# The place of projected tiles reused for residual rows, FFN weights and normed rows, and the second norm's tiles transposed by DMA instead of TensorE

## What is computed

```python
h_stream = h_stream + rms_norm(merged @ w_o[l], g_mix_post[l])
# ---- channel-mixing sub-layer: SwiGLU (sandwich norm) ----
h = rms_norm(h_stream, g_ffn_pre[l])
gate, up = jnp.split(h @ w_ffn_in[l], 2, axis=-1)
f = (jax.nn.silu(gate) * up) @ w_ffn_out[l]
h_stream = h_stream + rms_norm(f, g_ffn_post[l])
```

## Time and profile before

| | us |
|---|---|
| median of 3 runs (lowest, highest) | 1818.75 (1818.65, 1823.68) |
| the profiled execution's own time | 1814.77 |
| its span on the slowest core, core 2 | 1813.7 |
| PE busy in the span | 1747.8 (96%) |
| DVE, ACT, POOL busy | 692.9, 520.6, 122.1 |
| span of the fastest core, core 4 | 1797.7 |

### The profile page before, as it was taken

The page is one execution under the profiler, slowest core; times in us unless marked ns, Lnnn a source line. Parts: engine busy times, 40 slices in busy tenths (PEclk is TensorE's granted clock), DMA queues, the critical chain, the costliest instruction groups (busy, mean ns, idle before and its releaser), DMA issues.

```text
span 1813.7 us, 25284 instructions; the slowest of 8 cores (1797.7 to 1813.7 us)
## 1 busy us (share of the span) xinstructions
PE 1747.8 (96%) x9598; PEld 847.2 (47%) x9760; DVE 692.9 (38%) x825; ACT 520.6 (29%) x970; POOL 122.1 (7%) x262
## 2 busy tenths in 40 slices
PE   5999999999999989999899999999999999999998
PEld 3755555544444434444444444444444444444443
DVE  4666878967885634526610110101010110101023
ACT  5755566376547530024410000000000000101010
POOL 2000000000000011100000000000000000000000
PEclk9999999999999999999999999999999999999999
DMA  9753444466667889946954446455554431434456
GB/s 236 218 133 81 83 77 90 70 124 134 122 124 154 177 158 224 239 93 177 231 110 81 70 75 115 75 103 98 96 102 76 80 66 33 96 64 76 84 145 229
DMA packets 89239, 218.55 MB, mean 120 GB/s; under 512 B 34400, under 2 KB 35040, under 8 KB 83840
## 3 DMA queue, kind: packets, MB, share of 16 engines
q0 software_dynamic: 31744, 121.71, 39.5%
q1 hardware_dynamic: 54208, 90.06, 16.8%
q10 hardware_dynamic: 3168, 5.15, 0.8%
HBM read 302.28 MB, written 36.24 MB: 187 GB/s over the span
## 4 chain that ended last, share of the span: by engine, by line
PE 81%; DMA 10%; DVE 3%; issue 3%; SPq 2%; ACT 1%; ACTq 0%; DVEq 0%; POOLq 0%
PE ps L224 80%; DMA xin<-xseq 3%; DMA yr<-yc_d 3%; SPq L218 2%; DMA wr<-w_in 2%; DMA xr<-xseq 1%; DVE xs L251 1%; PE ps L232 1%; DVE ptmp L248 1%; DMA gT<-g_d 0%; ACT xs L242 0%; DVE os L251 0%; DMA g_d<-go 0%; DVE xg L251 0%; ACT xg L242 0%
## 5 line engine op out<-in xcount | busy, mean ns | idle before, releaser
L224 PE MATMUL ps<-hN,wf 128*128 128x512 bf16 x2759 | 606.8, 380 | 4.6 <-DVE hN L266 0.9
L224 PEld LDWEIGHTS ps<-hN,wf 128*128 128x128 bf16 x2816 | 275.8, 98 | 334.8 <-issue 4.3
L224 PE MATMUL ps<-hT,wr 128*128 128x512 bf16 (+1 forms) x1884 | 371.0, 350 | 8.6 <-DMA wr<-w_in 5.5
L224 PE MATMUL ps<-wfo,agr 128*128 128x512 bf16 x1379 | 302.5, 379 | 1.5
L248 DVE TENSOR_TENSOR agr<-ps,sgt 128x512 bf16<-128x512 f32 x88 | 60.8, 691 | 534.3 <-PE ps L224 530.9
L224 PEld LDWEIGHTS ps<-hT,wr 128*128 128x128 bf16 x1920 | 179.9, 97 | 176.0 <-issue 11.1
L224 PEld LDWEIGHTS ps<-wfo,agr 128*128 128x128 bf16 x1408 | 137.8, 98 | 166.1
L242 ACT ACTIVATE sgt<-ps 128x512 f32<-128x512 f32 x88 | 52.4, 597 | 537.9 <-PE ps L224 537.9
L224 PE MATMUL ps<-wo,mgd 128*128 128x512 bf16 x500 | 111.0, 379 | 2.0 <-ACT sg L244 0.9
L248 DVE TENSOR_TENSOR facc<-ps,gp2a 128x512 f32<-128x512 f32 x24 | 16.6, 692 | 212.2 <-ACT sqj L242 212.2
L242 ACT ACTIVATE sqj<-ps 128x512 bf16<-128x512 f32 x32 | 19.1, 597 | 271.5 <-PE ps L224 271.5
(11 more groups left out here) (152 smaller groups left out, 1367.9 us busy)
## 6 DMA issues: line engine op xcount, KB each, us to landing
wf<-w_ffn_in POOLq DMA_DIRECT2D x88, 512.0 KB, 5.8
wr<-w_in POOLq DMA_DIRECT2D x52, 512.0 KB, 6.0
wfo<-w_ffn_out POOLq DMA_DIRECT2D x16, 1408.0 KB, 9.6
xin<-xseq SPq DMA_DIRECT2D x15, 1024.0 KB, 8.4
wo<-w_o POOLq DMA_DIRECT2D x16, 512.0 KB, 14.2
yr<-yc_d SPq DMA_DIRECT2D x32, 256.0 KB, 11.1
xr<-xseq SPq DMA_DIRECT2D x16, 512.0 KB, 7.7
hs_d<-os SPq DMA_DIRECT2D x8, 1024.0 KB, 8.7
```

The costliest lines, as they stand in the source:

```text
L224: return lambda e: e.matmul(o, lhsT=l, rhs=r, start=st, stop=sp)
```

## The change

`mgd` is laid out by token tile, [128, 8, 16, 128], and known to the scheduler as eight regions `mg0` to `mg7`, so that the place of one token tile comes free when that tile is projected. A second residual buffer `xr1` takes the place of `mg0` and `mg1`, a third buffer of normed rows `xg2` that of `mg4`, two FFN weight buffers that of `mg2` and `mg3`, two more that of `gpost`. Of the nine `wf` buffers the first six loads take `wf5, wf6, wf3, wf4, wf7, wf8`, and the later ones `wf0` to `wf4` in turn. Token tile 7 uses `os3` instead of `os2`. The 16 TensorE transposes, the ACT copy and the DVE copy of each token tile are replaced by one DMA on SP's queue with `transpose=True`, for all eight tiles.

```diff
+FLIPPED = 8
...
+    def flip(self, out, in_, nbytes, slot, reads, writes):
+
+        self.add("sp", [lambda e: e.dma_start(out=out, in_=in_, transpose=True)], 0.4, reads, writes, dma=1.5 * nbytes, slot=slot)
...
-    mgd = S.tile("mgd", [128, 16, NTOK], BF16, 82112)
+    mgd = S.tile("mgd", [128, 8, 16, 128], BF16, 82112, parts=("mg", 8))
...
-            S.stt(mgd[:, m, cs], t[:], 0.5, YR[yi][:], ALU.mult, ALU.add, 512, [tk, "yr%d" % yi], [("mgd", m, blk)])
+            four = lambda v: v.rearrange("p (a n) -> p a n", a=4)
+            S.stt(mgd[:, 4 * blk:4 * blk + 4, m, :], four(t[:]), 0.5, four(YR[yi][:]), ALU.mult, ALU.add, 512, [tk, "yr%d" % yi],
+                  [("mg%d" % (4 * blk + i), m) for i in range(4)])
...
-    xr = S.tile("xr", [128, D], F32, 196800)
-    XG = [S.tile("xg%d" % i, [128, D], BF16, a) for i, a in enumerate((204992, 52288))]
+    XR = [S.tile("xr%d" % i, [128, D], F32, a) for i, a in enumerate((196800, 82112))]
+    XG = [S.tile("xg%d" % i, [128, D], BF16, a) for i, a in enumerate((204992, 52288, 98496))]
...
-        xg, xk = XG[(t + 1) % 2], "xg%d" % ((t + 1) % 2)
+        oi = 3 if t == 7 else t % 5
+        os_, ok = OS[oi], "os%d" % oi
+        xi = (1, 0, 1, 0, 2, 1, 0, 2)[t]
+        xg, xk = XG[xi], "xg%d" % xi
...
-        if t + 1 < 8:
-            load_r(t + 1)
+        if t + 2 < 8:
+            load_r(t + 2)
...
+        if t < FLIPPED:
+            S.flip(hN[:, :, 128 * t:128 * t + 128], xg[:], 524288, xk, [xk], [("hN", t, 0), ("hN", t, 1)])
+            return
         for h in range(2):
...
+    load_r(1)
     for t in range(8):
         if t >= 3 and t + 2 < 8:
...
-    WF = [S.tile("wf%d" % i, [128, 16, 128], BF16, 35904 + 4096 * i) for i in range(5)]
+    WF = [S.tile("wf%d" % i, [128, 16, 128], BF16, a) for i, a in enumerate((52288, 35904, 40000, 44096, 48192, 90304, 94400, 164032, 168128))]
...
-        i = fr[0] % 5
+        n = fr[0]
+        i = (5, 6, 3, 4, 7, 8)[n] if n < 6 else (n - 6) % 5
         fr[0] += 1
-        S.dma("pool", flat(WF[i][:]), src, 1048576, "wf%d" % i, writes=[("wf%d" % i,)])
+        S.dma("pool", flat(WF[i][:]), src, 1048576, "wf%d" % i, reads=[("hN", 2, 0)] if n < 6 else [], writes=[("wf%d" % i,)])
```

More of the change, by code:

```diff
@@ L66, in __init__, with region, tile @@
         self.sub = None
-    def tile(self, name, shape, dtype, addr):
+    def region(self, name, lo, hi):
+        self.inherit[name] = [n for (n, a, b) in self.tiles if a < hi and lo < b]
+        self.touch[name] = set()
+        self.tiles.append((name, lo, hi))
+    def tile(self, name, shape, dtype, addr, parts=None):
         nbytes = int(np.prod(shape[1:])) * (2 if dtype == BF16 else 4)
@@ L73, in tile @@
         assert name not in self.touch, name
-        self.inherit[name] = [n for (n, a, b) in self.tiles if a < hi and lo < b]
-        self.touch[name] = set()
-        self.tiles.append((name, lo, hi))
+        if parts is None:
+            self.region(name, lo, hi)
+        else:
+            for i in range(parts[1]):
+                self.region("%s%d" % (parts[0], i), lo + i * nbytes // parts[1], lo + (i + 1) * nbytes // parts[1])
         return self.nc.alloc_sbuf_tensor_at(name, list(shape), dtype, offset=LO + addr)
@@ L976, in _program @@
             q = 4 * nb + kq
-            after = ([("gs_d", EARLY[-3 + min(kq, 1)], 1)], [("g3", kq, 0)], [("mgd", 12 + kq, 0)], [("mgd", 15, 1)])[nb]
+            after = ([("gs_d", EARLY[-3 + min(kq, 1)], 1)], [("g3", kq, 0)], [("mg0", 12 + kq)], [("mg4", 15)])[nb]
             S.dma("pool", flat(WO[q][:]), w_o[nb][:, 2048 * kq:2048 * kq + 2048], 1048576, "wo%d" % q, reads=after, writes=["wo%d" % q])
@@ L981, in _program @@
     S.dma("sp", gpost[:], gains_d[1], 1048576, "gpost", writes=["gpost"])
-    S.dma("sp", gfpre[:], gains_d[2], 1048576, "gfpre", reads=[("mgd", 15, 0)], writes=["gfpre"])
+    S.dma("sp", gfpre[:], gains_d[2], 1048576, "gfpre", reads=[("mg0", 15)], writes=["gfpre"])
     OS = [S.tile("os%d" % i, [128, D], F32, a) for i, a in enumerate((180416, 188608, 56384, 35904, 44096))]
-    xr = S.tile("xr", [128, D], F32, 196800)
-    XG = [S.tile("xg%d" % i, [128, D], BF16, a) for i, a in enumerate((204992, 52288))]
+    XR = [S.tile("xr%d" % i, [128, D], F32, a) for i, a in enumerate((196800, 82112))]
+    XG = [S.tile("xg%d" % i, [128, D], BF16, a) for i, a in enumerate((204992, 52288, 98496))]
     hN = S.tile("hN", [128, 16, NTOK], BF16, 3072)
@@ L995, in project @@
     def project(t, nb):
-        os_, ok = OS[t % 5], "os%d" % (t % 5)
+        oi = 3 if t == 7 else t % 5
+        os_, ok = OS[oi], "os%d" % oi
         pb, pk = bank("all")
-        S.mms([(pb[:], mgd[:, k, 128 * t:128 * t + 128], WO[4 * nb + k // 4][:, k % 4, :], k == 0, k == 15, 512) for k in range(16)],
-              ["wo%d" % (4 * nb + kq) for kq in range(4)] + [("mgd", m, t // 4) for m in range(16)], [pk])
+        S.mms([(pb[:], mgd[:, t, k, :], WO[4 * nb + k // 4][:, k % 4, :], k == 0, k == 15, 512) for k in range(16)],
+              ["wo%d" % (4 * nb + kq) for kq in range(4)] + [("mg%d" % t, m) for m in range(16)], [pk])
         S.act(sqo[:], pb[:], AF.Square, 512, [pk], ["sqo", ("ssq", t, nb)], accum=ssq[:, 4 * t + nb:4 * t + nb + 1])
@@ L1005, in load_r @@
             hc = slice(1024 * h, 1024 * h + 1024)
-            S.dma("sp", xr[:, hc], xseq[16 + 128 * t:144 + 128 * t, hc], 524288, "xr%d" % h, writes=[("xr", h)])
+            S.dma("sp", XR[t % 2][:, hc], xseq[16 + 128 * t:144 + 128 * t, hc], 524288, "xr%d%d" % (t % 2, h), writes=[("xr%d" % (t % 2), h)])
     load_r(0)
     def finish(t):
-        os_, ok = OS[t % 5], "os%d" % (t % 5)
-        xg, xk = XG[(t + 1) % 2], "xg%d" % ((t + 1) % 2)
+        oi = 3 if t == 7 else t % 5
+        os_, ok = OS[oi], "os%d" % oi
+        xi = (1, 0, 1, 0, 2, 1, 0, 2)[t]
+        xg, xk = XG[xi], "xg%d" % xi
         OK = [(ok, nb) for nb in range(4)]
@@ L1019, in finish @@
             hc = slice(1024 * h, 1024 * h + 1024)
-            S.stt(os_[:, hc], os_[:, hc], r1, xr[:, hc], ALU.mult, ALU.add, 1024, OK[2 * h:2 * h + 2] + [r1k, ("xr", h)], OK[2 * h:2 * h + 2])
-        if t + 1 < 8:
-            load_r(t + 1)
+            S.stt(os_[:, hc], os_[:, hc], r1, XR[t % 2][:, hc], ALU.mult, ALU.add, 1024, OK[2 * h:2 * h + 2] + [r1k, ("xr%d" % (t % 2), h)], OK[2 * h:2 * h + 2])
+        if t + 2 < 8:
+            load_r(t + 2)
         S.dma("sp", hs_d[128 * t:128 * t + 128, :], os_[:], 1048576, ok, reads=OK, writes=[("hs_d", t)])
```

## The result

The changed kernel takes 1835.7 us (median of 6 runs, 1830.6 to 1836.2), the kernel before, run beside it, 1823.5; the ratio is **1.0074, 95% interval 1.0057 to 1.0091**, so 13.5 us (10 to 17) slower. Some executions run several per cent longer, with the cores of one die at a lower clock; the ratios leave these out, the median of 1823.5 doesn't. Forecast were +8.5 us, 1827, with 1811 to 1857 as range. The profiled execution took 1836.1 us, 21.4 more than the one of before, 1814.8; they lie at opposite ends of their runs, so the traces show a larger gap than the ratio.

What follows compares the result with a forecast made beforehand. PE, busy for 96% of the span, was taken to bound the kernel, with a nearly DMA-bound stretch before the FFN. Terms -20.2 + 27.0 + 1.7 = +8.5 us gave 1827 us on the median, range 1811 to 1857.

Steps and rivals of the forecast that it cites:

- -20.2 us beside the matmuls: From projection start to the `wfo` matmuls: 20.2 us of transposes, waits and half clock beside the matmuls, upper limit of the gain.
- PE solid to 873.8: In the projection: PE runs without pause from 763 until its 33rd group, the first needing transposed tiles, at 873.8 us.
- Stall of 27 us: At the first FFN group of blk 1: PE, needing tile 7 at 891.0, waits 27 us for its transposing DMA.
- own latency doesn't decide: Tile 7 before the FFN: its 11.1 us from sum to normed rows has it normed at about 886, so queued transfers decide.
- No wait for `xr` on DVE of over 2 us: Sign of being right: DVE never waits over 2 us for residual rows.
- q1's own work, 47.7 us: SP's queue after 822: seven tiles of residual loads and eight stores take 47.7 us, the middle of 44.0 and 51.4.
- The price T = 3.1 us: Transfer time of each of the eight transposing DMAs: 3.1 us, from 2,048 pieces of 256 bytes; bounds 1.5 to 6.3.
- SP's queue held: Possibility that issuing each transposing DMA holds SP's queue several us, so residual loads behind it slip; nothing bounded it.
- the much slower rival: Transposing DMAs at 6.3 us each or a held SP queue: stall 56.3 us, +37.8, 1857 us; chance 0.20, half beyond 1857.
- Clock +1.7: After the stall at the FFN's start: one drop of PE's clock costs 1.7 us, half of an earlier 3.4.
- The faster rival: Crossing as cheap as a copy, 1.5 us each, with a fuller queue: stall 10.3, sum -8.2, 1810.6 us; chance 0.20.
- Waits, at best 11.7 us: Between projection start and the `wfo` matmuls: removing waits for normed rows and other things, and half clock, gains at most 11.7 us.

## Why the prediction came out as it did

The direction was right, the size low by 5 us of the ratio's 13.5, and the main mechanism (PE is cleared, and what it gains comes back as a stall on the transfers at the start of the FFN) is what the trace shows. Point by point:

- *-20.2 us beside the matmuls* and *PE solid to 873.8*: right on the slowest core, PE is solid to 872.4. But 20.2 is the worst of eight cores; the others had 13.9 to 17.6, so less to gain. The matmuls with `wfo` start at 1522.84, so (1522.84 - 761.76) - 718.3 = 42.8 us now lie where 20.2 were. They are 37.9 us of waits and 4.9 of half clock and gaps.
- *Stall of 27 us*: sized low on the slowest core, 37.9, and right for the others (23 to 32). **The step that failed** is that PE has one wait, for tile 7, and that tile 7's "own latency doesn't decide". The second half of its residual rows was issued only at 881.3, behind the DMAs of tiles 3 and 4 on the held queue (16.4 and 7.3 us); DVE waited 11.1 us for it, until 893.2. Its square stood behind the FFN's first `sgt` on ACT, until 905.9. It was normed at 912.1 instead of 886. From its issue it took 18.3 us to land, where the sum has T + 2 = 5.1, and it landed at 930.5, where I had 918. "No wait for `xr` on DVE of over 2 us" was a sign of being right that failed: 11.1 us here, 7.5 to 12.4 over the eight cores.
- *q1's own work, 47.7 us*: 3.7 us were taken off for `hsb` and gains, but these were issued at 904.2 and 907.1, so hardly any of their 1.3 MB lies before 908. The rate is 55.1 us for 15.7 MB, 3.5 us per MB and not 3.3, some 4 us more at the upper end. This isn't what failed.
- *The price T = 3.1 us*: about right in the mean. With its queue alone it is 25 ns a piece, 2,048 x 25 / 16 = 3.2 us. Over the kernel, q1's share rose from 16.8% to 18.2%, 29 us for eight, 3.7 each; the pieces by themselves add up to 3.4 to 4.2 each over the eight cores, and to 2.4 to 2.6 as plain copies. The size of the piece, 256 bytes, was right too, but from the wrong reason: I took it from the destination's runs, and it stays with unbroken ones. That this price is what decides between rivals is borne out: pieces alone are 11 of the 20 us.
- *SP's queue held*: I gave this, in the much slower rival, as something that nothing bounds. It happened, 1.4 to 16.4 us each on core 1, and it made the loads of `xr` slip, but it did not lead to 1857. That PE had to wait for the same transfers anyway is my reading and isn't shown. The 1865.7 us with loads on POOL's queue are no example of it, since nothing stood behind the held queue there.
- *Clock +1.7*: sized low. I counted one drop, there are two. PE's granted clock is 0.50, the 1.2 GHz level, in the wait, and 0.74 and 0.83 in the 12 us behind each: 0.26 x 12 = 3.1 us after the first wait and 0.17 x 12 = 2.0 after the second.
- *The faster rival* (T as a plain copy's, 1810.6) was tried with 4 KB copies: 0.9991, and 0.9980 with own semaphores. Even at a copy's price the crossing does no better than TensorE's transposes, 0.9962.
- *Waits, at best 11.7 us*: the second residual buffer alone is worth 0.9962 against 1.0014, 0.5% or 9 us; that it "hides the latency of a load, not its transfer" undersold it. DVE's waits for `xr` are 7.3 to 15.6 us over the cores before, 1 to 3 us with two buffers and no transposing DMA, and 7.5 to 12.4 in the changed kernel: the held queue takes the buffer's gain back. It needs no transposing DMA, and I hadn't asked what the change would be worth without them.
- The rule of the Trainium skill in "Advanced Engine Details and Errata", section X-Bar Transpose (TRN2), that such DMAs are as fast as regular ones, at 350 to 400 GB/s, isn't met here: 0.524 MB in 3.2 us of 16 engines is 164 GB/s alone, and in the run without stores all queues together moved 85 GB/s beside weight loads on core 3. Against plain copies in the same 256-byte pieces it comes close, 21 against 20 ns a piece with nothing beside them; with copies in 4 KB pieces the kernel takes 0.9991, against 1.0074. The Trainium skill's "DMA: Bandwidth & Descriptors", section Latency and other measured facts, gives 261 GB/s with a non-contiguous middle dimension, 2.0 us by an estimate from that page; no run here reaches it, with broken or unbroken runs.

Shares of the 20 us by the runs' ratios: TensorE to 4 KB copies +0.29% (5 us), 4 KB to 256-byte pieces +0.63% (11 us), copying to transposing +0.20% (4 us; 0.4 to 0.5% with the two versions with own semaphores). The intervals are 0.1 to 0.25% wide on each side, so only the middle one stands clearly by itself. The traces bear the order out. Take on each core the time from the start of the projection to the first matmul with `wfo`, less the 718.3 us of its matmuls. In the median of the eight cores of one execution that is 14.3 us before, 12.7 without transposing DMAs, 16.0 with 4 KB copies, 27.2 with 256-byte copies and 31.1 with transposing DMAs, steps of 3, 11 and 4 us. With one residual buffer and no transposing DMA it is 17.6, 5 us more than with two and 3 more than before, which is less than the 9 us of the ratios.

## What to carry to other kernels

Here a transpose moved from a full PE to DMA was paid in a stretch where the DMA engines were full already. Count its pieces and not its bytes, and look at what stands behind it on the issuing queue. Small pieces held that queue whether they transposed or not. Before moving work off an engine that waits, remove what it waits for: the second residual buffer alone brought 0.5%, and the version without any transposing DMA is the one to keep. A wait that vanishes when semaphores are separated may only move; look where the next one ends before calling it a cost.

## What was unexpected in the hardware

- A transposing DMA of 128 x 2048 bf16, SBUF to SBUF, goes as 2,048 pieces of 256 bytes whether its destination is broken or not (51,040 packets under 512 bytes in both layouts), at 25 ns a piece with its queue alone.
- Beside other packets its pieces get slower: in the mean 63 ns beside loads on POOL's queue and 51 beside stores and residual loads, against 21 alone. In the two stretches shown they took 88 and 172 ns, and the load's packets 874 and 519 instead of 328; landing went from a median of 5.5 us (846 to 852) to 33.6 (870 to 906). Plain copies in pieces of the same size stay at 20 ns. A few pieces of over 500 ns make the difference, and once they took 548 ns in the mean with hardly any other traffic. What in the chip they contend for wasn't found.
- The queue that issues it is held meanwhile, 1.4 to 57.7 us. A plain copy in 256-byte pieces takes 0.6 us in the median, but what stands behind it is held up to 14.0 us on core 6: SP's issues add up to 58 to 64 us a core with such copies, to 72 to 77 with transposing DMAs and to 13 to 15 with 4 KB copies.
